# A diffusion layer's expert stage: 32 of the 384 dense tokens get their activations from gathered weight rows

## What is computed

```python
best, pos = lax.top_k(cand, PEER_TOPK)            # per token: 8 heads x 16 of 16384 experts
gate = jax.nn.softmax(best, -1)
def block(args):
    tb, eb, gb = args                             # tokens, expert numbers, gates
    ub = jnp.take(u_emb, eb, axis=0)
    vb = jnp.take(v_emb, eb, axis=0)
    act = jax.nn.gelu(jnp.einsum('td,ted->te', tb, ub), approximate=False) * gb
    return jnp.einsum('te,ted->td', act, vb)
```

## Time and profile before

| | |
|---|---|
| median of 3 runs | 3439.09 us (3437.67 to 3448.2) |
| the profiled execution's own time | 3448.69 us |
| its span | 3446.8 us |
| TensorE busy | 3374.7 us, 98% |
| VectorE, ScalarE, GpSimd busy | 2144.5, 1186.6, 1849.8 us |
| DMA | 874.71 MB, mean 254 GB/s |
| mean granted TensorE clock | 0.992 |

### The profile page before, as it was taken

The page is one execution under the profiler, slowest core; times in us unless marked ns, Lnnn a source line. Parts: engine busy times, 40 slices in busy tenths (PEclk is TensorE's granted clock), DMA queues, the critical chain, the costliest instruction groups (busy, mean ns, idle before and its releaser), DMA issues.

```text
span 3446.8 us, 44031 instructions
## 1 busy us (share of the span) xinstructions
PE 3374.7 (98%) x16931; PEld 2934.1 (85%) x16931; DVE 2144.5 (62%) x3280; ACT 1186.6 (34%) x1632; POOL 1849.8 (54%) x904
## 2 busy tenths in 40 slices
PE   7999999999999999999999999999999999999998
PEld 4688888766788899999999999999788888888887
DVE  2388887746414759993766676654566565566556
ACT  3322221234123232233555555543223233232223
POOL 1210001213444445776666666666788788787875
PEclk8999999999999999999999999999999999999999
DMA  9656642565423236777677767778978878878972
GB/s 384 255 185 205 218 165 107 182 225 205 160 98 147 88 126 243 287 270 277 256 315 301 293 268 299 313 312 320 354 281 349 335 295 336 345 290 327 357 270 108
DMA packets 184618, 874.71 MB, mean 254 GB/s; under 512 B 16621, under 2 KB 77501, under 8 KB 97844
## 3 DMA queue, kind: packets, MB, share of 16 engines
q1 hardware_dynamic: 122160, 525.38, 41.3%
q0 software_dynamic: 38688, 281.15, 20.3%
q10 hardware_dynamic: 23652, 66.69, 5.1%
HBM read 803.78 MB, written 69.32 MB: 253 GB/s over the span
## 4 chain that ended last, share of the span: by engine, by line
PE 90%; DVE 5%; DMA 3%; POOL 1%; ACT 1%; issue 0%; ACTq 0%; SPq 0%; DVEq 0%; POOLq 0%
PE bank L2120 84%; PE bank L2381 2%; DMA ring<-in_w_mod 1%; PE bank L2498 1%; PE bank L2355 1%; DMA ring<-in_v_emb 1%; POOL low L765 1%; PE bank L2128 1%; PE bank L2481 0%; DVE low L1436 0%; DMA rows_b<-in_v_rows,small 0%; DVE b L1880 0%; POOL split L807 0%; PE bank L2445 0%; DVE gate_w L1654 0%
## 5 line engine op out<-in xcount | busy, mean ns | idle before, releaser
L807 POOL TENSOR_TENSOR split<-ring,split 128x1024 fp32r<-128x1024 f32 x544 | 1356.7, 2504 | 650.8 <-ACT split L1145 650.0
L2120 PE MATMUL bank<-h_hi,split 128*128 128x384 f32 (+1 forms) x4608 | 1220.7, 341 | 6.9 <-POOL split L807 5.8
L1145 ACT ACTIVATE split<-ring 128x1024 fp32r<-128x1024 f32 x544 | 573.9, 1060 | 1418.2 <-PE bank L2120 1257.4
L2120 PE MATMUL bank<-split,a_split 128*128 128x512 f32 x4608 | 1047.6, 390 | 3.9 <-DVE acc L1992 2.3
L2120 PEld LDWEIGHTS bank<-split,a_split 128*128 128x128 f32 x4608 | 865.6, 188 | 185.6 <-DVE acc L1992 2.7
L2120 PEld LDWEIGHTS bank<-h_hi,split 128*128 128x128 f32 x4608 | 838.6, 188 | 27.8 <-POOL split L807 6.9
L2120 PE MATMUL bank<-h_lo,split 128*128 128x384 f32 (+1 forms) x2304 | 784.8, 341 | 0.0
L2120 PEld LDWEIGHTS bank<-h_lo,split 128*128 128x128 f32 x2304 | 433.2, 188 | 9.5
L2120 PE MATMUL bank<-hT_hi,w_hi 128*128 128x512 f32 (+1 forms) x768 | 289.5, 377 | 5.3 <-POOL ring_lo L727 2.2
L2120 PE MATMUL bank<-hT_lo,w_hi 128*128 128x512 f32 (+1 forms) x768 | 287.0, 374 | 0.0
L2120 PE MATMUL bank<-hT_hi,ring_lo 128*128 128x512 f32 (+1 forms) x704 | 260.4, 370 | 0.0
(11 more groups left out here) (318 smaller groups left out, 3858.2 us busy)
## 6 DMA issues: line engine op xcount, KB each, us to landing
ring<-in_u_emb SPq DMA_DIRECT2D x128, 1024.0 KB
ring<-in_v_emb SPq DMA_DIRECT2D x128, 1024.0 KB
ring<-in_w_mod SPq DMA_DIRECT2D x48, 1024.0 KB
ring<-in_w_in SPq DMA_DIRECT2D x44, 1024.0 KB
ring<-in_w_mod SPq DMA_DIRECT2D x64, 512.0 KB, 4.5
neurons<-tiny ACTq DMA_DIRECT2D x128, 192.0 KB
gate_table<-b ACTq DMA_DIRECT2D x6, 4096.0 KB, 15.1
weigh<-neurons SPq DMA_DIRECT2D x32, 768.0 KB
```

Source lines behind the costliest of these rows:

```text
L807: nc.gpsimd.tensor_tensor(split[:, r % 2, 1, at].bitcast(F32R), ring[:, r % 4, :, :].rearrange("p k n -> p (k n)")[:, at], split[:, r % 2, ...
L1145: nc.scalar.activation(split[:, q % 2, 0, at].bitcast(F32R), ring[:, q, :, :].rearrange("p k n -> p (k n)")[:, at], ACT.Copy)\
L2120: last = mm(out_, left[a].bitcast(F32R), right[b].bitcast(F32R), start=start and n == 0, stop=stop and n == 2)
```

## The change

The last 32 of the 384 dense tokens (`EXTRA`) leave the neuron matmuls, which then have 352 columns (`TN`). Their 32 x 128 activations are spread over 128 partitions (four copies of the 32 tokens, each with 32 of the 128 expert places), so that 32 more gathers and dots make them. Before these, a plain load and two copies bring the tokens' activations to where the dot reads them, and after them two copies and a load bring back those of the last tile: 162 row visits in place of 128. The activations, transposed, are multiplied into the gates of these tokens before the last table chunk is made, and the neuron store holds the constant 1 in their columns, so the sums stay as they are (36 matmuls of 512 columns).

To make the 352 columns one access pattern, `h2_hi` and `h2_lo` are laid out in runs of 32 columns in place of 128. The visits have a new timetable (`ROW_UNIT`). Dots up to unit 125 as before, but two a unit from unit 116 and four at unit 126; 25 more in sum units 0 to 19; then the 128 sets of `v` rows in sum units 22 to 116, one or two a unit, none in each eighth. They use five buffers: two slices of `x2_dense` are added, which is loaded in sum unit 118 instead of 0. Gathers before unit 44 come one unit later than before.

```diff
+EXTRA = 32
+EG = P // EXTRA
+TN = TD - EXTRA
+E_LOAD = 57
+E_ROWS = range(E_LOAD + 1, E_LOAD + 1 + EXTRA)
+T_LOAD = E_LOAD + 1 + EXTRA
+U_ROWS = SLOTS + 2 + EXTRA
+ALL_ROWS = U_ROWS + SLOTS
...
+def row_units():
+    at = list(range(3, PRE))
+    for unit in range(PRE, NK - 2):
+        at += [unit] * (2 if unit >= PRE + CHUNKS * CHUNK_UNITS else 1)
+    at += [NK - 2] * 4
+    unit = NK
+    while len(at) < U_ROWS:
+        if unit % 8 != 7:
+            at += [unit] * min(1 + unit % 2, U_ROWS - len(at))
+        unit += 1
+    units = [u for u in range(unit + 2, 2 * NK - 11) if u % 8 != 7]
+    return at + [units[m * len(units) // SLOTS] for m in range(SLOTS)]
...
-            h2_hi = region("h2_hi", 8192, search)[:, :].rearrange("p (j k t) -> p k j t", j=LT, t=P)
+            h2_hi = region("h2_hi", 8192, search)[:, :].rearrange("p (g k t) -> p k g t", k=KT, t=EXTRA)
...
-        gathered_rows = [rows_a, rows_b, rows_c]
+        gathered_rows = [rows_a, rows_b, rows_c, x2_dense[:, 0, :], x2_dense[:, 1, :]]
...
                 if n >= 3:
-                    pool.wait_ge(rows_used, n - 2)
+                    pool.wait_ge(rows_used, max(0, ROW_EARLIER[n]) + 1)
...
             for r in range(1, V0 + NK):
                 rest_half(r, 0)
                 rest_half(r, 1)
-                if 0 <= r - (U0 + 2) < SLOTS:
-                    gather_rows(r - (U0 + 2))
-                for m in range(SLOTS):
-                    if V0 + 3 + m - m // 8 == r:
-                        gather_rows(SLOTS + m)
+                for n in range(ALL_ROWS):
+                    if U0 + ROW_UNIT[n] - (PRE <= ROW_UNIT[n] < NK - 12) == r:
+                        gather_rows(n)
...
-                nc.scalar.activation(neuron_out[:, q % 2, :], bank[:, 4 + q % 2, 0:TD], ACT.Gelu)\
+                nc.scalar.activation(neuron_out[:, q % 2, 0:TN], bank[:, 4 + q % 2, 0:TN], ACT.Gelu)\
...
+                if r == 4:
+                    act.wait_ge(h2_made, 2)
+                    act.dma_start(tile_dram[:, :], h2_sparse).then_inc(e_moved, 16)
+                    for g in range(EG):
+                        act.dma_start(extra_dram[g * EXTRA:(g + 1) * EXTRA, :], sh2_row[extra, :]).then_inc(e_moved, 16)
...
+                if k == 8:
+                    nc.vector.scalar_tensor_tensor(sc2_row[extra, :], x2[extra, JD - 1, :], rstd2[extra, JD - 1:JD],
+                                                   sc2_row[extra, :], ALU.mult, ALU.mult).then_inc(a2_made, 1)
+                if k == 10:
+                    dve.wait_ge(a2_made, 9)
+                    nc.vector.tensor_tensor(sh2_row[extra, :], sc2_row[extra, :], sh2_row[extra, :], ALU.add)\
+                        .then_inc(h2_made, 1)
...
+                if n in (E_LOAD, T_LOAD):
+                    dve.wait_ge(rows_used, n)
+                    rows = gathered_rows[ROW_PLACE[n]]
+                    nc.vector.tensor_copy(bank_rows[:, 0:D - P], rows[:, 0:D - P])
+                    nc.vector.tensor_copy(h2_last, rows[:, D - P:D]).then_inc(rows_used, 1)
...
+                if unit == E_UNIT + 3:
+                    dve.wait_ge(nval_gelu, 1)
+                    nc.vector.transpose(act_e, nval_e).then_inc(act_made, 1)
...
+            first = ROW_UNIT.index(NK - 2)
             weigh_group(0)
-            dot(NK - 5)
+            dot(first)
+            dot(first + 1)
             rest_group(0)
             weigh_group(1)
             rest_group(1)
-            dot(NK - 4)
-            rows_added = 0
+            dot(first + 2)
+            dot(first + 3)
...
                     for k in range(h * 8, h * 8 + 8):
-                        last = mm3(bank[:, 4 + q % 2, 0:TD].rearrange("p (j t) -> p j t", t=P),
+                        last = mm3(bank[:, 4 + q % 2, 0:TN].rearrange("p (g t) -> p g t", t=EXTRA),
                                    [split[:, q % 2, w, k * P:(k + 1) * P] for w in range(2)],
-                                   [h2_hi[:, k, 0:JD, :], h2_lo[:, k, 0:JD, :]], k == 0, k == KT - 1)
+                                   [h2_hi[:, k, 0:TN // EXTRA, :], h2_lo[:, k, 0:TN // EXTRA, :]], k == 0, k == KT - 1)
```

More of the change, by code:

```diff
@@ L1359, in _ @@
                            .then_inc(last_rows, 16)
-            with act.Fori(1, GROUPS // 2 - 1) as i:
-                for k in range(8):
-                    sweep_unit(i * 8 + k, k % 4, (k - 6, i * 2 + (k - 4)) if k > 5 else None)
+                if unit == NK - 10:
+                    act.wait_ge(rows_used, ALL_ROWS)
+                    act.wait_ge(last_rows, 16 * (1 + LT))
+                    for j in range(JD):
+                        act.dma_start(x2_dense[:, j, :], x2_dram[j * P:(j + 1) * P, :]).then_inc(last_rows, 16)
             for k in range(6):
@@ L1963, in _ @@
             for unit in range(PRE + CHUNKS * CHUNK_UNITS, NK - 2):
-                dot(unit - 3)
+                dots(unit)
             def weigh_group(g):
@@ L2046, in _ @@
                     rest_group(g + 1)
+                if unit == NK - 7:
+                    dve.wait_ge(last_rows, 16 * (JD + 1 + LT))
                 flush_here(unit, 0)
```

158 lines of the change are left out of this document (110 added, 48 removed).

## The result

Before 3440.81 us, after 3473.42 us (medians of 4 runs each, side by side); ratio 1.0092, 95% interval 1.0070 to 1.0114. The forecast was 3374, its range 3354 to 3408. The profiled execution of the changed kernel took 3469.24 us and has a span of 3467.4 us.

What follows compares the result with a forecast made beforehand. TensorE, busy 98% of the span, was taken as the bound. Columns -81.9, search +1, loop's end +8 net and sums +8 gave -64.9 us, so the median goes from 3439.09 to 3374 us, range 3354 to 3408.

Steps and rivals of the forecast that it cites:

- columns: Neuron matmuls: 352 columns take 160.2 ns, 13.3 ns less, over 6144 matmuls; 81.9 us off.
- The shorter runs: Neuron and query matmuls: reading the moving operand in runs of 32 costs zero, at most 1.6 us.
- Runs cost: Rival, neuron and query matmuls: each run start beyond the third takes time; at 3 ns each 3550 us, slower; 3%.
- The search: Search: VectorE's dots come at times TensorE does not set, a faster TensorE meets them; 1 us lost, 0 to 5.
- So this lies in idle time: Neuron loop and sums: VectorE's 34 added visits, 88 us, fit in its idle time and cost nothing.
- Table chunks: Table stage: clearing the bank after a chunk's store fits by 2 to 3 us; 0 lost, up to 5.
- The loop's end: End of neuron loop: paired gathers from unit 116 and four at unit 126 cost 12 us, between 2 and 18.
- The 3.9 us of before go away: Change of loops: TensorE's former waits of 3.9 us vanish as `x2_dense`'s 3 MB leaves this place.
- The sums: Sums: denser gathers delay the ring load behind SyncE's wait for `a_split_made`; 8 us lost, 0 to 31.
- The transfers bind: Rival: twelve cycles of the sums late by 2.6 us each, the loop's end by 18; 3403 us; 20%.
- Weight loads bind: Rival, neuron matmuls: weight loads of 188 ns hold the slot, narrower matmuls gain nothing; 3456 us, slower; 3%.
- the line: Matmul time by columns: 0.416 ns each plus a fixed 13.9 ns, checked at 256 columns.

Runs made afterwards that it cites:

- spread: Changed kernel with eight extra visits moved into units 69 to 111 and 13 gathers, not 20, in units 116 to 125; 3470.8 us, ratio 1.0068.
- thin_adds: Changed kernel with VectorE's dots and additions from unit 116 on working on 32 columns in place of 2048, all transfers kept; 3443.0 us, ratio 0.9992.
- one_run: Changed kernel with a chunk's 352 dense columns in one run, a query matmul's other 160 as a second matmul; 3478.0 us, ratio 1.0081.

## Where the prediction failed

In us of the spans, by its own steps; the third column sums to the 20.6 by which the spans differ. (The medians differ by 32.6: the profiled execution of the kernel before stood 7.9 us above its median, that of the changed one 4.2 below.) The prediction's 8 net for the loop's end is 12 less 3.9 that lie behind it, at the change of loops; here the 3.9 stand with the sums, where the ledger has them:

| step | predicted | measured |
|---|---|---|
| columns | -81.9 | -54.7 |
| runs of 32 in the query | 0 | +8.8 |
| search | +1 | +13.2 |
| table chunks | 0 | +0.3 |
| loop's end | +12 | +23.1 |
| change of loops and sums | +4.1 | +34.3 |
| before the search | 0 | -4.4 |

Measured, the columns are 6144 x 8.9 ns. Each other row is what its stretch lost beside the new pace, with the neuron matmuls that the trace has in it: the search 6.0 us gained (1270.90 to 1654.6 before, 1274.80 to 1652.5 after) of 2160 x 8.9 ns = 19.2, the table stage 29.4 of 29.7 (3338 matmuls), the end 17.8 lost where 600 matmuls should gain 5.3. The last row is the 3.9 us by which unit 1 started later, less the 8.8 of the query, and 0.4 that unit 0 gained. It is no gain of the change: 4.2 us of it are there before the query, ahead of a piece of the mixer that the change doesn't touch (kernel before, changed kernel):

```profile
915.26 141.68 PE bank L2120 x624
```

```profile
911.08 141.68 PE bank L2236 x624
```

**The waits cost more than their length.** In the loop's end TensorE waited 18.5 us, yet 23.1 are lost. The stretch, before and after (us; busy PE, PEld, DVE, ACT, POOL; PEclk, DMA share, GB/s):

```profile
2278.80:2382.90 104.10, 104.10 (x603) 104.10 (x602) 43.42 (x52) 33.84 (x39) 74.60 (x37) 1.00 0.87 338
```

```profile
2247.30:2369.20 121.90, 103.44 (x602) 101.75 (x602) 84.55 (x92) 30.88 (x37) 81.86 (x48) 0.93 0.98 390
```

Its 600 matmuls at 164.6 ns are 98.8 us, and TensorE was busy for 103.44. The granted clock (PEclk) tells why; 1.00 is 2.4 GHz, 0.50 is 1.2. After TensorE's longest wait it reads 0.50, and two matmuls take 0.59 us (2360.55 to 2361.14) in place of 0.33:

```profile
2357.00:2362.00 5.00, 2.17 (x7) 2.20 (x8) 3.11 (x3) 0.00 (x0) 4.98 (x4) 0.50 1.01 420
```

```profile
2359.83 0.63 PE L2236 MATMUL bank<-h_hi,split 128*128 128x352 f32 x1 [11.31 <-POOL split L851]
2360.26 0.49 PE L2236 MATMUL bank<-h_lo,split 128*128 128x352 f32 x1
2360.55 0.79 PE L2236 MATMUL bank<-h_hi,split 128*128 128x352 f32 x2
2361.14 0.49 PE L2236 MATMUL bank<-h_lo,split 128*128 128x352 f32 x1
```

The table stage of spread has the same, against that of the changed kernel: 12.9 us more busy time, beside the 19.5 of waits.

```profile
1652.60:2279.80 627.20, 607.66 (x3721) 604.39 (x3720) 447.61 (x784) 349.83 (x681) 405.62 (x216) 0.98 0.77 300
```

```profile
1652.50:2247.30 594.80, 594.80 (x3722) 594.52 (x3721) 427.18 (x752) 350.68 (x681) 398.17 (x208) 1.00 0.77 302
```

Of the 34.3 us of the sums 23.0 are waits (26.9 in place of 3.9, mostly for GpSimd and VectorE) and 11.3 are busy time for the same 4608 matmuls. How much of the 11.3 is the clock wasn't parted. The prediction counted each wait at its length.

- **The shorter runs: "I take zero", bound 1.6 us.** The largest single miss, 27 + 9 us. The bound was drawn from runs of 128 and scaled by the count of starts. But where a cost is hidden under another, three starts at nothing say nothing of eleven. The rival *Runs cost* had the nearer mechanism. It took the price for additive from the fourth run on, and said that 1.7 ns a start would eat the columns' gain; the eight more starts cost 4.4 ns, 0.55 each.
- **The search, 1 us lost: VectorE's dots "come at times that TensorE does not set".** They come at times that GpSimd sets. The operations between them stretch with GpSimd's halves, and the dots release those halves. The faster TensorE was bought with waits of 14.8 us, not 6.6, and VectorE full where it had 9 us in 60.
- **"So this lies in idle time"** (88 us of visits on VectorE) took busy time for the only measure. VectorE did have idle time in the sums (194.45 us busy of 300), but its work sets when SyncE issues and when buffers come free: without its work on all row sets from unit 116 on, the 32 extra ones among them, half of the loss of both stretches goes (thin_adds).
- **Table chunks, 0**, was right, and so was the margin named: spread overdrew it.
- **The loop's end, 12 gross.** Right in mechanism (20 + 4 gathers, GpSimd behind dots, transfers that don't fit), low in size: 17.8 us longer than before, 23.1 beside the pace of the units. The prediction left most of the bandwidth deficit to the ring's lead. But the 4 MB store of the last chunk was on its way too, issued at 2251.9 and landed after 21.9 us (before 16.9), and the DMA share is 0.98 over the stretch. A gather issued at 2255.20 had its dot at 2274.31, 19.1 us later in place of the 7.8 of the earlier trace rows, and GpSimd stood 12.92 us:

```profile
2255.20 0.96 POOL L886 DMA_INDIRECT rows_b<-in_u_rows,small  x1
...
2276.96 0.94 POOL L886 DMA_INDIRECT rows_b<-in_u_rows,small  x1 [12.92 <-DVE tiny L1908]
```

- **"The 3.9 us of before go away"** with the 3 MB at the change of loops. They didn't: from 2385 to 2550 us TensorE waited 5.0 us, for VectorE's flushes.
- **The sums, 8 of at most 31.** The step pointed at the right place, the ring load behind `a_split_made`, and took the nearer end for its 4.1 us of margin. That margin was of one cycle. With the wait itself made later (5.22 us for the split, where the kernel before has a median of 2.20) and the load behind 1.5 MB in a fuller machine (10.3 us to ScalarE's start in the earlier trace rows, 21.4 now), TensorE waited for GpSimd 16 times in 13 cycles. The waits stayed under the bound of 31, the stretch passed it.
- *The transfers bind*, 20%, was the nearest rival (3403), and still short: it lacked the runs and the search. *Weight loads bind*, 3%: one_run shows that narrow matmuls do leave the line, at 113 ns, well below the 160 of a neuron matmul.
- **The range.** "Its own terms hold the forecast within 3362 to 3392" is too narrow for the bounds given: all at their low ends make 3355, all at their high ends (runs 1.6, search 5, chunks 5, end 18, sums 31) 3414. The measured 3473 lies outside these too, so the terms failed and not only the range.

## What to carry to other kernels

A cost measured at zero can't be scaled: ask first what hides it, and at which count the cover ends. Before calling an engine's time idle, look at the least, median and longest duration of its operations by where their operands lie; here a wide spread was another engine's work. Count a long wait of TensorE at more than its length, if the granted clock falls behind it. And before blaming a transfer for its bytes, see what its queue was waiting for: moving one load ahead of one wait gave back 25 of 34 us with every byte kept.

## What the runs showed of the hardware that was new to me

- Moving operands in runs of 32 fp32 columns take 14.8 to 15.0 ns a run, at 352, 384 and 512 columns alike, with no fixed part; runs of 64 show nothing. Three runs of 118 take 163.3 ns, 2 more than the line.
- Matmuls of 160 columns with a weight load each, between matmuls of 352, take 113 ns on average; four of 256 columns follow at 120 ns.
- VectorE's `tensor_tensor` of 512 columns goes from 0.69 us to 5.5 beside two halves of GpSimd's subtraction if both operands lie in SBUF, and stays within 17 ns if one is in PSUM (180 operations).
- After TensorE had stood for 11.3 us, the granted clock read 0.50 and its matmuls of 352 columns followed at 0.29 us in place of 0.164.
- A 1 MB ring load landed after 4.8 us in the neuron loop and 14.8 in the sums (medians), at DMA shares of 0.79 (1900 to 2000 us) and 0.85 (2550 to 3400).
